# One block for the projection and the delta rule, the last solve batch spread over the first chunks, and the decoder's mask waits moved to its transpositions

## The reference

```python
def gated_deltanet(h, w_in, conv_w, a_log, dt_bias, o_gain, w_out):
    proj = h @ w_in
    qkv, z, a, b = jnp.split(proj, [...], axis=-1)
    qkv = causal_dwconv_silu(qkv, conv_w)
    ...
    o = gated_delta_rule(q, k, v, g, beta)
    o = rms_norm(o, o_gain).astype(h.dtype).reshape(bsz, seq, A_V)
    return (o * jax.nn.silu(z)) @ w_out

# in gated_delta_rule, for every chunk:
    a_strict = jnp.tril(jnp.einsum('nbhid,nbhjd->nbhij', k_beta, k_c) * decay, -1)
    sol = lax.linalg.triangular_solve(a_strict + jnp.eye(A_CHUNK), rhs, left_side=True, lower=True, unit_diagonal=True)
    ...
    def step(state, inp):
        v_new = u_i - jnp.einsum('bhck,bhkv->bhcv', w_i, state)
        o_i = einsum(q_i * exp(g_i), state) + einsum(qk_i, v_new)
        state = state * exp(g_last) + einsum(k_i * exp(g_last - g_i), v_new)
        return state, o_i
```

## Time and profile before

| what | us |
|---|---|
| median of 3 runs | 3161.34 (3160.24 to 3176.55) |
| profiled execution | 3155.64 |
| its span, from the first to the last instruction | 3153.9 |
| PE busy | 3023.0 (96%) |
| DVE busy | 1737.2 (55%) |
| ACT busy | 1236.5 (39%) |
| POOL busy | 718.0 (23%) |
| mean DMA rate over the span | 136 GB/s |

### The profile page before, as it was taken

One profiled execution on the slowest core, in us unless ns is written; L12 is line 12 of the kernel. 1 busy time (PEld: TensorE's weight loads), 2 busy tenths in 40 slices (PEclk: granted clock), 3 DMA queues, 4 the chain that ended last, 5 costly groups with the idle time before them and its releaser, 6 DMA issues.

```text
span 3153.9 us, 39919 instructions
## 1 busy us (share of the span) xinstructions
PE 3023.0 (96%) x15148; PEld 2283.6 (72%) x15148; DVE 1737.2 (55%) x2759; ACT 1236.5 (39%) x2161; POOL 718.0 (23%) x596
## 2 busy tenths in 40 slices
PE   6999999999968997999999999999999999999998
PEld 5777777888857886888878888886555555555687
DVE  5666654657645666555313221104877777778543
ACT  5455555444314555334212202210544444445411
POOL 0000001232235453000000000001545544555300
PEclk9999999999989998999999999999999999999999
DMA  6344423767555674557534421126254342331243
GB/s 229 109 140 140 140 76 98 232 206 218 181 151 192 228 233 143 169 174 223 147 102 98 132 81 74 74 74 172 60 141 115 97 113 70 91 95 52 93 146 121
DMA packets 291083, 428.04 MB, mean 136 GB/s; under 512 B 74654, under 2 KB 187942, under 8 KB 285756
## 3 DMA queue, kind: packets, MB, share of 16 engines
q1 hardware_dynamic: 261612, 359.19, 38.0%
q0 software_dynamic: 13168, 50.42, 5.0%
q10 hardware_dynamic: 16112, 15.86, 1.9%
HBM read 274.58 MB, written 150.69 MB: 135 GB/s over the span
## 4 chain that ended last, share of the span: by engine, by line
PE 56%; ACTq 1%; DVE 1%; issue 1%; ACT 1%; POOL 0%; DMA 0%; DVEq 0%; SPq 0%; POOLq 0%
PE at_ps L1879 8%; PE at_ps L1930 6%; PE at_ps L1782 6%; PE at_ps L1917 6%; PE at_ps L1784 6%; PE at_ps L1783 6%; PE at_ps L1861 5%; PE at_ps L1864 4%; PE at_ps L1847 3%; PE at_ps L1795 2%; PE at_ps L1796 2%; PE at_ps L1797 2%; ACTq L2382 1%; PE at_ps L1893 1%; ACT at_probs L2479 1%
## 5 line engine op out<-in xcount | busy, mean ns | idle before, releaser
L2479 ACT ACTIVATE at_probs<-at_ps 128x512 f32<-128x512 f32 (+3 forms) x640 | 331.7, 534 | 337.7 <-PE at_ps L1864 270.9
L2103 DVE TENSOR_REDUCE at_partial<-at_ps 128x1 f32<-128x512 f32 (+3 forms) x640 | 370.8, 605 | 141.2 <-PE at_ps L1847 109.0
L106 PE MATMUL pa_y<-pa_h_high,pa_w_high 128*128 128x512 f32 x992 | 395.0, 398 | 0.0
L108 PE MATMUL pa_y<-pa_h_high,pa_w_low 128*128 128x512 f32 x992 | 386.4, 390 | 0.0
L107 PE MATMUL pa_y<-pa_h_low,pa_w_high 128*128 128x512 f32 x992 | 386.2, 389 | 0.0
L1559 POOL TENSOR_TENSOR at_plain<-at_plain,at_probs 128x512 f32<-128x512 f32 (+3 forms) x256 | 310.2, 1212 | 225.4 <-ACT at_probs L2479 209.7
L1782 PE MATMUL at_ps<-at_h_high,at_w_high 128*128 128x512 f32 x768 | 299.6, 390 | 1.0 <-DVE at_w_low L2032 0.9
L1783 PE MATMUL at_ps<-at_h_low,at_w_high 128*128 128x512 f32 x768 | 298.8, 389 | 0.0
L1784 PE MATMUL at_ps<-at_h_high,at_w_low 128*128 128x512 f32 x768 | 298.8, 389 | 0.0
L1861 PE MATMUL at_ps<-at_h_low,at_h_high 67*128 67x512 f32 (+3 forms) x640 | 260.3, 407 | 12.4 <-ACT at_probs L2479 12.2
L1864 PE MATMUL at_ps<-at_h_low,at_h_high 128*128 128x512 f32 (+3 forms) x640 | 252.7, 395 | 0.0
(11 more groups left out here) (350 smaller groups left out, 5300.2 us busy)
## 6 DMA issues: line engine op xcount, KB each, us to landing
at_h_low<-s_Q SPq DMA_DIRECT2D x96, 256.0 KB, 6.8
s_qkv<-pa_acc POOLq DMA_DIRECT2D x16, 1024.0 KB, 9.9
pa_sil<-s_qkv SPq DMA_DIRECT2D x16, 1024.0 KB, 7.0
dr_kv<-s_qkv SPq DMA_DIRECT2D x16, 1024.0 KB, 8.8
s_Q<-at_parts SPq DMA_DIRECT2D x64, 256.0 KB, 4.1
at_h_high<-s_K SPq DMA_DIRECT2D x32, 512.0 KB, 5.5
pa_wraw<-in_a_w_in_dram ACTq DMA_DIRECT2D x15, 1024.0 KB, 6.4
s_qkv<-pa_sil POOLq DMA_DIRECT2D x8, 1024.0 KB, 6.1
```

Source lines behind the costliest of these rows:

```text
L106: nc.tensor.matmul(out, w_high[:, k], h_high[:, k], start=k == 0, stop=False)
L108: ins = nc.tensor.matmul(out, w_low[:, k], h_high[:, k], start=False, stop=k == KC - 1)
L2103: reduced.done(v.tensor_reduce(partial[:, u % 2, h * NQ + sub, grp:grp + 1], rough[:, j % 3, 0:width], AX.X, ALU.max))
L2479: probs_ok.done(a.activation(probs[:, R % 2, t, h, off:BLK], logits[:, l % 3, off:BLK], ACT.Exp))
```

## The change

The stages pa and dr become one block: `delta_rule` no longer opens a block but returns functions for each engine, which `deltanet_projection` calls from within its own loops or behind them. The barrier between the two goes; waits on single semaphores take its place. The tiles of the delta rule are laid over those of the projection in such a way that M, the columns, kv0, the masks and one set of work matrices lie where the projection's buffers are free early (acc, sil, sq, the gate buffers), kv2 lies on ybuf, and the rest on the projection's inputs h, free when PE has finished. Accordingly SP loads M(0), columns, gain, kv0 and M(1) behind the load of the last solve batch; q0, kv1 and q1 when PE has finished; and z0, z1, kv2 and M(2) when the last z is stored. z gets semaphores of its own. POOL's masks and the assembly for chunk 0 go to tile 31, block 2, DVE's masks and the first turning of blocks to tile 30, block 2, and PE's prologue merges right behind the last tile. The turning of chunk 1's blocks moves behind the prologue's last corners.

Of the last solve batch DVE makes three parts in the projection (steps 1 to 17) and four at the start of chunks 1 to 4; SP stores it at chunk 6 and waits for that store before M(12).

In the decoder the two waits go from ahead of the first product to the first transposition.

```diff
+    def beside(self, name):
+
+        other = Stage(self.nc, name)
+        other.sems = self.sems
+        return other
...
-        ybuf, acc = st.sb("ybuf", [P, 3 + SEQ]), st.sb("acc", [P, SEQ])
-        sil, sq = st.sb("sil", [P, SEQ]), st.sb("sq", [P, SEQ])
+        delta = following(st.beside("dr"))
         with nc.sbuf_tensor("pa_w_mod", [P, KC, 2 * D], F32) as w_mod:
             pass
         h_high, h_low = (st.sb(n, [P, KC, SEQ], F32R) for n in ("h_high", "h_low"))
+        ybuf, acc = st.sb("ybuf", [P, 3 + SEQ]), st.sb("acc", [P, SEQ])
+        sil, sq = st.sb("sil", [P, SEQ]), st.sb("sq", [P, SEQ])
...
             load_batch(3)
-            store_batch(3)
             sp.wait_ge(cols_stored, 16)
-            sp.wait_ge(x_stored, 64 * BATCHES)
             sp.wait_ge(m_stored, 48 * NC)
+            sp.wait_ge(late_stored, 16 * V)
+            for mark in (qkg_ok, qh_ok, pt_ok):
+                mark.wait(sp, NC - 1, 1)
+            delta.sync_first(sp)
             sp.wait_ge(pt_stored, 16 * NC)
             for s in range(2):
                 sp.wait_ge(qh_stored[s], 16 * NC // 2)
+            projected(sp)
+            delta.sync_second(sp)
+            sp.wait_ge(late_stored, 16 * (TILES - QK))
+            delta.sync(sp, lambda: store_batch(BATCHES - 1), lambda: sp.wait_ge(x_stored, 64 * BATCHES))
...
-            pool.wait_ge(late_stored, 16 * (TILES - QK))
+                    if (T, n) == (TILES - 1, 2):
+                        pool.wait_ge(pt_stored, 16 * NC)
+                        for s in range(2):
+                            pool.wait_ge(qh_stored[s], 16 * NC // 2)
+                        pool.wait_ge(d_stored, 64 * NC)
+                        pool.wait_ge(m_stored, 48 * NC)
+                        pool.wait_ge(w_split, TILES)
+                        delta.gpsimd_first(pool)
+            projected(pool)
+            delta.gpsimd(pool)
...
+            for mark in (b_ok, pt_ok):
+                mark.wait(pe, NC - 1, 1)
+            delta.tensor_first(pe)
+            bank_free.wait(pe, TILES - 1, NB - 1)
+            delta.tensor(pe)
...
-                cuts = (1, 7, 14, 22, SB - 1)
+                cuts = (1, 7, 14, 22, SB - 1) if b < BATCHES - 1 else (1, 7, 14, 18, 21, 24, 27, SB - 1)
                 if part == 0:
                     begun.wait(dve, b)
                 for m in range(cuts[part], cuts[part + 1]):
                     eliminate(m)
-                if part == 3:
+                if part == len(cuts) - 2:
                     solved.wait()
                     xt_ok.done(v.tensor_copy(Bd[:, :, :], X[:, :, :].rearrange("p i j -> p j i")))
+
+            def solve_rest(c):
+
+                if 1 <= c <= 4:
+                    solve_part(BATCHES - 1, c + 2)
...
+                    if (T, n) == (TILES - 2, 2):
+                        dve.wait_ge(d_stored, 64 * NC)
+                        dve.wait_ge(m_stored, 48 * NC)
+                        delta.vector_first(dve)
                     for at, b in SOLVE_AT.items():
-                        if at <= q < at + 4:
+                        if at <= q < at + (4 if b < BATCHES - 1 else 3):
                             solve_part(b, q - at)
+                    if (T, n) == (TILES - 2, 2):
+                        delta.vector_second(dve)
+            projected(dve)
+            delta.vector(dve, solve_rest)
...
+            delta.scalar(act)
+    return delta.fetched
...
+    with st.ctx:
+        fetched = Fetched(nc, st.ctx, "oa", s_uT, w_out)
+        many = lambda names, shape: [st.sb(n, shape) for n in names.split()]
+        qh, PT, z = (many(f"{n}0 {n}1", [P, AH, C]) for n in ("qh", "PT", "z"))
+        kv1, Z5, Z6 = st.sb("kv1", [P, 2 * AH, C]), st.sb("Z5", [P, HG, P]), st.sb("Z6", [P, HG, P])
+        k_hat, bv = (many(f"{n}0 {n}1", [P, AH, C]) for n in ("k_hat", "bv"))
+        R, VN, S, sq, rt, U = many("R VN S sq rt U", [P, AH, C])
+        work1 = many("WB51 R51 T131 WB61 R61 W61", [P, HG, P])
+        kv2 = st.sb("kv2", [P, 2 * AH, C])
+        st.sb("ybuf_rest", [P, 3])
+        M = many("M0 M1", [P, MW])
+        cols, kv0 = st.sb("cols", [P, 4, NC, AH]), st.sb("kv0", [P, 2 * AH, C])
+        kv = [kv0, kv1, kv2]
...
+        def load_q(sp, c):
+            s = c % 2
+            sp.dma_start(qh[s][:, :, :], s_qh[c]).then_inc(q_in[s], 16)
+            sp.dma_start(PT[s][:, :, :], s_PT[c]).then_inc(q_in[s], 16)
+
+        def load_z(sp, c):
+            sp.dma_start(z[c % 2][:, :, :], s_z[c]).then_inc(z_in[c % 2], 16)
+
+        def sync_first(sp):
+
+            load_m(sp, 0)
+            sp.dma_start(cols[:, :, :, :].rearrange("p k c h -> p k (c h)"), s_cols).then_inc(consts_in, 16)
+            sp.dma_start(gain[:, :], o_gain).then_inc(consts_in, 16)
+            load_kv(sp, 0)
+            load_m(sp, 1)
+
+        def sync_second(sp):
+
+            load_q(sp, 0)
+            load_kv(sp, 1)
+            load_q(sp, 1)
+
+        def sync(sp, store_last_batch, wait_last_batch):
...
+            for c in range(2):
+                load_z(sp, c)
+            load_kv(sp, 2)
             for c in range(-1, NC):
+                if c == 6:
+                    store_last_batch()
                 if c + 3 < NC:
                     six_ok.wait(sp, c + 1)
                     diag_ok.wait(sp, c + 1)
-                    load_m(c + 3)
+                    if c + 3 == NC - 4:
+                        wait_last_batch()
+                    load_m(sp, c + 3)
                 if 1 <= c < NC - 1:
                     ga_ok.wait(sp, c - 1, 1)
-                    load_q(c + 1)
+                    load_q(sp, c + 1)
+                    load_z(sp, c + 1)
                 if 0 <= c < NC - 3:
                     ks_ok.wait(sp, c, 1)
-                    load_kv(c + 3)
+                    load_kv(sp, c + 3)
...
+        def gpsimd_first(pool):
...
+            assemble(pool, 0)
+
+        def gpsimd(pool):
+            for f in range(1, NC):
+                assemble(pool, f)
...
+        def tensor_first(pe):
             pe.wait_ge(pool_set, 2)
             pe.wait_ge(dve_set, 3)
-            first_merge(0, -1)
-            second_merge(0, -1)
-            last_merge(0)
+            first_merge(pe, 0, -1)
+            second_merge(pe, 0, -1)
+            last_merge(pe, 0)
+
+        def tensor(pe):
+            pe.wait_ge(dve_set, 4)
             for c in range(NC):
                 f = c + 1 if c + 1 < NC else None
-                state_products(c)
+                state_products(pe, c)
...
+        def vector_second(dve):
+
+            turn_blocks(dve, 0)
             dve.wait_ge(consts_in, 32)
             dve.sem_inc(dve_set, 1)
 
-            def turn_blocks(f):
-                s = f % 2
-                dve.wait_ge(m_in[s], 16 * 11 * (f // 2 + 1))
-                six_ok.wait(dve, f - 2)
-                mt_ok.done(v.transpose(MT[s][:, :], M[s][:, P:3 * P]))
+        def vector(dve, beside):
+            v = nc.vector
+            stt = v.scalar_tensor_tensor
+            v.memset(S[:, :, :], 0.0).then_inc(dve_set, 1)
...
-            turn_blocks(0)
-            turn_blocks(1)
             first_corners(0)
             second_corners(0)
             values(0)
             last_corners(0)
+            turn_blocks(dve, 1)
             for c in range(NC):
                 f = c + 1 if c + 1 < NC else None
+                beside(c)
...
                 xn_ok.wait(pe, c)
+                if c == 0:
+                    pe.wait_ge(masks_set, 1)
+                    pe.wait_ge(carry_ok, NB - 1)
                 xT_ok.wait(pe, c - 2)
                 for k in range(KC):
                     ins = nc.tensor.transpose(turned1[c % 2][:, row_at(k)], xn[:, c % 2, row_at(k)], ident[:, :])
@@ -1952,8 +2041,6 @@
                         if n == 0 and t == 1:
                             turn(NT - 1)
 
-            pe.wait_ge(masks_set, 1)
-            pe.wait_ge(carry_ok, NB - 1)
...
+    following = lambda st: delta_rule(nc, st, s_qkv, s_z, s_cols, s_qh, s_PT, s_X, s_B5, s_B6, a["o_gain_col"], s_uT, a["a_w_out"][0])
+    fetched = deltanet_projection(nc, a["x"][0], a["c_cols"], mods, s_mod, a["a_pre_cols"], a["a_w_in"][0], a["taps"], a["gate_cols"], s_qkv, s_z, s_abT, s_G, s_cols,
+                        s_qh, s_PT, s_D, s_X, s_B5, s_B6, following)
     s_x1, s_xnT1 = dram("s_x1", (SEQ, D)), dram("s_xnT", (D, SEQ))
-    with ExitStack() as ctx:
-        fetched = Fetched(nc, ctx, "oa", s_uT, a["a_w_out"][0])
-        delta_rule(nc, s_qkv, s_z, s_cols, s_qh, s_PT, s_X, s_B5, s_B6, a["o_gain_col"], s_uT, fetched)
```

More of the change, by code:

```diff
@@ L14 @@
 import itertools
+from collections import namedtuple
 import math
@@ new lines, in solve, with second_merge @@
+        def solve(pe, c):
+            l6_out.wait(pe, c)
+            for g in range(2):
+                r_ok.wait(pe, c, g)
+                for h in heads(g):
+                    ins = mm(at_head(psA, g, h), TT[c % 2][:, h], R[:, h], start=True, stop=True)
+                tr_ok.done(ins)
```

(31 more changed lines are left out.)

279 lines of the change are left out of this document (113 added, 166 removed).

## The result

The change made the kernel faster, by half of what I had forecast: 3146.99 us (median of 6, 3142.91 to 3157.01) against 3163.44 for the kernel before on the same chip, a ratio of 0.9948 with a 95% interval of 0.9923 to 0.9973, or -16.4 us where -33.7 was forecast. 3146.99 lies 5 us above the range of 3117 to 3142.

A forecast was written before the change was run, and what follows sets the result against it. PE is busy over 96% of the span, so only its two holes, before the delta rule's loop and at the decoder's start, can give time: -25.4 + 1.0 - 9.3 = -33.7, from 3161.34 to 3128, range 3117 to 3142.

The forecast's parts named there:

- The change doesn't do what it says: Rival: M(0)'s loads stay behind something ending with the projections, decoder's start unchanged; only 11 us gained, 3150; 6%.
- First boundary, -25.4: Projection to delta rule's chunk loop: M(2)'s arrival sets the loop, at 930.6 instead of 955.98; between -29.1 and -18.1.
- the z store: Last store of z, queued behind POOL's products: issued at 910.6, lands 9.0 later at 919.6; SP waits for it.
- The bound of 14.2: Slow limit for the last z store: the slowest z transfer of this stretch, behind 5 MB, took 14.2 us.
- M(2)'s eleven issues: SP's loads of M(2) after the z store: 6.8 us of issuing plus 1.0 of full queue.
- the bound of 6.8 + 3.1: Slow limit for issuing M(2)'s loads: 6.8 us plus 3.1 (two fifths of 7.8) of full queue.
- My second rival: Late z store, DVE and POOL blocking each other, full queue: M(2) at 941.4, -22.9 in all, 3138; 15%.
- The prologue, 9.1: Ahead of chunk 0: takes the same 9.1 us as before the change, so chunk 0 starts at 916.8, 25.9 earlier.
- The rest of the solve, +1.0: Solve parts 3 to 6, moved to chunks 1 to 4, overrun DVE's idle time: +1.0, between 0 and 1.5.
- four issues (0.6 each, as M's): Last solve batch's store on SP in chunk 6: hidden by 4.9 us of waiting, 0; 2.4 without this cover.
- My fifth rival: Slower: the chunk loop becomes bound by the store of U, 3.5 us more in each of 15 chunks; 3180; 4%.
- Second boundary, -9.3: Decoder's start: PE begins at the first weight split, 1249.6 against 1258.99, not after POOL's masks; between -9.4 and -6.

The follow-up runs named there:

- the fitted kernels: Kernel after with csil moved behind the projection's weights, 3133.85, ratio 0.9899; the same move with M(2)'s loads ahead and the solve's stores spread, 3133.11, then 3122.07.

## Why the prediction was wrong, point by point

**What failed was a part of the change that had no term.** The swap of two lines of allocations stood in the diff, and I costed it at nothing, without saying so: my sum begins with the projection's end at 907.7 as if that could not move. It moved by 15.7 us in the profile, and by 15.5 by the ratios of the kernels with and without the rest of 32 bytes, since each of the projection's products follows the last at 234 ns instead of 227. None of the rivals had it. "The change doesn't do what it says" was the nearest in time (3150), by another mechanism: both places do what they say. With this one cost taken out the change gives 3133.85, 6 us above the forecast and inside the range.

**First boundary, -25.4: the mechanism right, the size -21.1.** M(2) is 27.9 us behind the projection's end, where I had 22.9. The terms that I had read off rows came out: POOL's products end 2.1 behind the projection (2.9 forecast), three loads 1.4 (1.3), the landing 2.1 (1.9), chunk 1 another 11.4 (12.1). The two that I had worked out did not. From its issue the z store took 12.2 to SP's next load, not 9.0: the rate of 407 GB/s was that of 3 us, and 4.2 MB in the time from 923.71 to 937.81 make 298 here. The bound of 14.2 held. And M(2)'s eleven issues took 10.0, not 6.8 + 1.0, one of them blocked for 3.19; the bound of 6.8 + 3.1 was just missed. My second rival had the store at 14.2, the full queue at 3.1 (3.2 came) and part 2 of the solve at its whole 3.5, M(2) at 941.4, and so -14.6 for this boundary: -21.1 lies between it and the forecast, nearer to the forecast.

**DVE and POOL do hold each other up, and DVE pays for it.** POOL's products took some 0.15 us longer each beside the solve, 1.1 us in all, not up to 3.5. DVE lost 10.8: part 2 took 14.4 us instead of 3.55, one operation to each POOL product, the two together 1.41, where alone they follow each other at some 1.25 and 0.44. The prediction had the sign of it, 1.35 instead of 0.4, and left it out with the words "in them DVE loses the most, so that the sum leaves it out". The Trainium skill, page "SBUF — State Buffer", section "SBUF: two separate sides", says that of a GpSimd instruction that reads SBUF and a DVE operation with two SBUF inputs, the one that starts first takes the shared ports for its whole length and the other fully blocks. The trace agrees in that each DVE operation waits for most of a product; it differs in that the two take 1.41 and not their sum, 1.69.

**The prologue, 9.1, took 11.8**, and that cost nothing. DVE's loss is what I had put at nothing here: the first corners are queued on DVE behind part 2, which so ended 6 us behind the projection. M(2) set the loop either way, as the run with part 2 moved shows.

**The rest of the solve, +1.0: +2.4.** Chunks 1 to 5 together take nearly what they took before (96.9 against 96.4); chunk 6 alone is 3.5 longer. The step at fault is "four issues (0.6 each, as M's)", hidden by SP's 4.9 us of waiting. They took 7.24. The trace of before had the same four issues at four other places, at 3.17, 3.92, 7.89 and 2.96; I priced them by another DMA. The longest of these:

```profile
872.61 7.89 SPq L318 DMA_DIRECT2D s_X<-pa_Bd  x4
```

My fifth rival's mechanism, a late store of U, is what this cost is, in one chunk instead of fifteen.

**Second boundary, -9.3: -9.25**, and 9.4 in the profile of the run that undoes it. The wait is ended by DVE's split, 10.47 (some 9.5 forecast), and the transposition has no wait.

## What to carry to other kernels

Moving a tile is an edit with a price: look at which tiles a product reads together, and compare the duration of the same instruction before and after, first of all, before looking for waits. Price a moved DMA by the rows of that DMA, a transfer by the rate of a stretch as long as it, not by the best one, and work that comes to lie beside another engine's by rows in which the two run beside each other: part 2 of the solve took four times its time. And where one queue feeds every stage, a wait that is taken away is followed by the next in that queue: of 5.7 us gained in chunk 1 nothing came through.

## What had not been expected of the hardware

A float32r product of 128x512 follows the last at 227 ns where its weights start, by the sizes in the code, a multiple of 256 bytes behind its moving operand (before, the fitted kernels) and at 234 ns with a rest of 32 (after, and the kernel before with a pad); with rests of 64 and 128 its median duration is 394 and 393 ns, like the 395 of the rest of 32, against 389. In the decoder of the kernel after the rest is zero (where it starts, h_low lies 65,536 bytes behind h_high, and both are cut at multiples of 512), and it is 226 there: 15 products in 3.56 us, (3.56 - 0.39) / 14.

```profile
1299.68 3.56 PE L2016 MATMUL at_ps<-at_h_low,at_h_high 128*128 128x512 f32 x15
```

Other rests, other types, and where in the chip it arises were not tried. Of the 20 us that 2,976 products x 6.7 ns make, 15.7 show at the projection's end; PE's wait for the loads of pa_sil, 4.6 us before and 2.5 after, took up 2, and where the rest went was not followed.
